# Query weights of the expert heads loaded ahead, and gathers that take row places in the order in which they come free

## The chip, the cores and the metric

The kernel runs on one core of a Trainium2 chip. Its engines run programs of their own and meet at semaphores: TensorE (PE, matrix products), VectorE (DVE), ScalarE (ACT), GpSimd (POOL) and SyncE (SP), which here only issues DMAs. The DMA engines (16 for the core) move data between the chip's memory (HBM) and on-chip memory. The metric is the device time of one execution in microseconds (us); lower is better.

## The reference, cut to what matters

Two transformer blocks run over 256 tokens of width 1024 in float32. The change touches only the end of the second block, a feed-forward layer that picks single experts (PEER): eight heads, each of which chooses 16 of 16384 experts for every token.

```python
P_HEADS, N_KEYS, P_KEY_DIM, P_TOPK, P_CHUNK = 8, 128, 256, 16, 128

def peer_ffn(x, w_q, sub_keys, expert_u, expert_v):
    q = _rms((xt @ w_q).reshape(T, P_HEADS, P_KEY_DIM))
    s1 = einsum('thd,hnd->thn', q[..., :half], sub_keys[:, 0])
    s2 = einsum('thd,hnd->thn', q[..., half:], sub_keys[:, 1])
    v1, i1 = top_k(s1, P_TOPK)
    v2, i2 = top_k(s2, P_TOPK)
    cand = (v1[..., :, None] + v2[..., None, :]).reshape(T, P_HEADS, P_TOPK * P_TOPK)
    vals, ci = top_k(cand, P_TOPK)
    e = take(i1, ci // P_TOPK) * N_KEYS + take(i2, ci % P_TOPK)
    g = softmax(vals)
    a = einsum('cd,ckd->ck', xc, expert_u[ec])
    w = g * gelu(a)
    return einsum('ck,ckd->cd', w, expert_v[ec])
```

`h + peer_ffn(rmsnorm(h))` is the output.

## The kernel before, in words

The blocks ahead of the expert layer stay as they are. In the expert layer the work is cut into 16 **units**: unit u belongs to head u // 2 and to tile t = u % 2 of 128 tokens. A unit has 16 **rows**: row k is one gather, an indirect DMA that POOL issues and that brings, for each of 128 tokens, the 8 KB of its k-th expert (the vectors u and v side by side, `peer_uv`): 1 MB. A row goes through the engines so: VectorE takes the dot product of its u part with the tokens (`dot`, L2880); after four rows ScalarE makes the gelu (`gelu_of`, L1695) and VectorE the weights (`weights_of`, L2890); ScalarE scales an identity matrix by each weight (`diagonals`, L1683); PE multiplies it with the v part and adds it up in PSUM (`add_experts`, L949), and signals `v_used`.

A row lies in one of 16 **places** of 2048 floats per partition (`slots`): 0 and 13 to 15 in arena_u, 1 in uv_proj, 2 and 3 in uv_mk, 4 to 7 in ring, 8, 11 and 12 in arena_v, 9 and 10 in uv_gain. Before, row k of every unit lies in place k, so the gather of row k waits for row k of the unit before. Places 4 to 7 hold the output projection's weights until PE signals `w_out_used` (twice, one count for two places), place 12 the sub-keys until they are turned, place 8 the first head's query weights.

The choice of experts for unit u + 1 is made on VectorE between the dot products of unit u (`first_eights` to `name_experts`), and `experts_ready` lets POOL issue its gathers. For a head's first tile it needs the scores of the next head: PE computes the queries of that head for both tiles from its **query weights** (1 MB, `peer_wq`), ScalarE copies and squares them, PE makes sums of squares and key scores (`key_scores`, L934, L939, after row 5 of an even unit), VectorE signals `ms_ready`, and POOL makes the scale (`power`, L1905) after its gather of row 9 of the odd unit.

Query weights: the first head's go to place 8; those of heads 1 to 3 (`early_wq`) to places 13 to 15, loaded before the layer begins, and PE computes the queries of all three (`early_queries`, L919) before its first row, which frees these places for rows 13 to 15 of unit 0. Heads 4 to 7 share one region of arena_v that is no place (`late_wq`): SP loads the next after PE has used the last (`late_wq_used`, L490), and PE computes their queries in units 6, 8, 10 and 12 (`key_queries`). PE and ScalarE write out the first six units and run units 6 to 13 as a loop; VectorE and POOL write out two and run 2 to 13 as a loop; the last two are written out.

Order is set by each engine's program alone: POOL issues gathers in order of rows, and whatever a gather waits for holds up all that stands behind it on POOL.

## Time and profile before

| | us |
|---|---|
| median of 3 runs | 1421.2 (1420.14 to 1421.49) |
| the profiled execution | 1421.38 |
| its span, first to last instruction | 1419.6 |
| first gather issued | 759.30 |
| dot product of the last row | 1412.00 |
| PE busy | 1295.4 (91%) |
| VectorE busy | 952.7 (67%) |
| ScalarE busy | 548.9 (39%) |
| POOL busy | 371.1 (26%) |

The profile is of one execution. "x4" after a line counts the instructions that it merges; a bracket at its end says how long the engine stood idle before and what ended that. PE's products in float32 are recorded in two passes, so one row is four records. "From issue to landing" of a DMA is the time until its data has arrived. Line numbers are those of the kernel before.

### The profile page before, as it was taken

What the parts mean: (1) busy time and instruction counts of PE and PEld (TensorE: products, weight loads), DVE (VectorE), ACT (ScalarE), POOL (GpSimd) and SP (SyncE); (2) the same over time, 40 slices, a digit from 0 to 9 for tenths busy, and PEclk for the clock granted to TensorE, in tenths of its full rate; (3) what the DMA queues carried; (4) which work ended last, traced back from release to release, by engine and by line L of the source; (5) the groups of instructions that cost most, each with busy time, mean ns of one, the idle gap of its engine ahead of it and who ended that gap; (6) DMA issues with size and microseconds to landing.
All of it is one profiled execution on the core that took longest, in us unless ns stands there. A gap on an engine that the chain in (4) does not pass through costs nothing.

```text
span 1419.6 us, 18216 instructions
## 1 busy us (share of the span) xinstructions
PE 1295.4 (91%) x5858; PEld 882.7 (62%) x5858; DVE 952.7 (67%) x2302; ACT 548.9 (39%) x1135; POOL 371.1 (26%) x392
## 2 busy tenths in 40 slices
PE   7999999999999999999999988887878879788778
PEld 6998888878978888878776633333433435343333
DVE  4577566675676665685746787777767677777755
ACT  4674444445655444455742322212222222122221
POOL 0104000000000000012804455444444444434440
PEclk9999999999999999999999999899999999999999
DMA  9815665546325565465335999999999999999997
GB/s 358 307 63 160 195 194 177 177 149 240 116 90 178 178 190 194 159 227 175 121 119 223 420 420 421 420 422 422 422 420 421 422 421 421 422 422 421 421 421 306
DMA packets 96962, 406.63 MB, mean 286 GB/s; under 512 B 6891, under 2 KB 43948, under 8 KB 60172
## 3 DMA queue, kind: packets, MB, share of 16 engines
q0 software_dynamic: 39552, 276.60, 47.4%
q1 hardware_dynamic: 57356, 129.34, 26.6%
q8 instruction: 31, 0.51, 0.1%
q14 instruction: 23, 0.19, 0.0%
HBM read 404.84 MB, written 1.07 MB: 286 GB/s over the span
## 4 chain that ended last, share of the span: by engine, by line
PE 54%; DMA 23%; DVE 9%; issue 8%; POOL 4%; ACT 2%; DVEq 0%; SPq 0%; POOLq 0%; ACTq 0%
DMA uv_proj<-in_peer_uv,prob 17%; PE ps_up L835 8%; PE ps L775 6%; PE ps L949 6%; PE ps L776 6%; PE ps L777 6%; PE ps_up L837 4%; DMA arena_u<-in_peer_uv,prob 3%; PE ps_up L775 3%; PE ps_up L777 3%; PE ps_up L776 3%; PE ps L1019 2%; DMA ring<-in_peer_uv,prob 2%; PE ps_up L919 1%; POOL small L1905 1%
## 5 line engine op out<-in xcount | busy, mean ns | idle before, releaser
L2177 DVE TENSOR_TENSOR w_low<-ring,w_high 128x1024 fp32r<-128x1024 f32 x140 | 165.3, 1221 | 47.2 <-ACT w_high L1367 39.9
L835 PE MATMUL ps_up<-hT_both,w_high 128*128 128x512 f32 x512 | 182.2, 399 | 0.9 <-DVE hT_both L2170 0.9
L949 PE MATMUL ps<-arena_u,sco 128*128 128x512 f32 x256 | 131.9, 663 | 39.5 <-ACT sco L1683 39.5
L1367 ACT ACTIVATE w_high<-ring 128x1024 fp32r<-128x1024 f32 x140 | 140.3, 1052 | 69.9 <-PE ps L777 69.9
L949 PE MATMUL ps<-arena_v,sco 128*128 128x512 f32 x192 | 101.0, 654 | 48.0 <-ACT sco L1683 48.0
L1683 ACT ACTIVATE sco<-const,prob 128x128 f32<-128x128 f32 x256 | 85.2, 392 | 153.1 <-DVE prob L2890 129.3
L837 PE MATMUL ps_up<-hT_both,w_low 128*128 128x256 f32 x512 | 143.8, 281 | 0.0
L1695 ACT ACTIVATE prob<-prob 128x4 f32<-128x4 f32 (+2 forms) x67 | 13.8, 206 | 319.5 <-DVE prob L2880 319.5
L1911 POOL TENSOR_SCALAR small<-small 128x1 f32<-128x1 f32 x8 | 4.2, 525 | 485.6 <-ACT arena_v L1399 485.4
L949 PE MATMUL ps<-ring,sco 128*128 128x512 f32 x256 | 117.9, 610 | 9.8 <-ACT sco L1683 9.8
L2880 DVE CUSTOM_DVE_ANT_0 arena_u<-arena_u,nat 128x1024 f32<-128x1024 f32 x64 | 78.0, 1225 | 67.6 <-DMA arena_u<-in_peer_uv,prob 67.6
L949 PEld LDWEIGHTS ps<-arena_u,sco 128*128 128x128 f32 x256 | 52.7, 210 | 109.8 <-issue 60.5
L2086 POOL DMA_INDIRECT arena_u<-in_peer_uv,prob x64 | 73.6, 1150 | 169.5 <-PE ps L949 119.7
L835 PEld LDWEIGHTS ps_up<-hT_both,w_high 128*128 128x128 f32 x512 | 96.2, 188 | 24.9 <-DVE hT_both L2170 1.3
L949 PEld LDWEIGHTS ps<-arena_v,sco 128*128 128x128 f32 x192 | 36.7, 202 | 105.2 <-ACT sco L1683 69.4
L837 PEld LDWEIGHTS ps_up<-hT_both,w_low 128*128 128x128 f32 x512 | 96.6, 189 | 1.2
L775 PE MATMUL ps<-w_high,act_high 128*128 128x512 f32 x240 | 94.5, 394 | 0.0
L776 PE MATMUL ps<-w_low,act_high 128*128 128x512 f32 x240 | 94.1, 392 | 0.0
L949 PEld LDWEIGHTS ps<-ring,sco 128*128 128x128 f32 x256 | 48.6, 195 | 73.0 <-issue 54.2
L777 PE MATMUL ps<-w_high,act_low 128*128 128x512 f32 x240 | 93.7, 390 | 0.0
L2880 DVE CUSTOM_DVE_ANT_0 arena_v<-arena_v,nat 128x1024 f32<-128x1024 f32 x48 | 58.6, 1224 | 43.0 <-DMA arena_v<-in_peer_uv,prob 43.0
L2880 DVE CUSTOM_DVE_ANT_0 ring<-ring,nat 128x1024 f32<-128x1024 f32 x64 | 78.4, 1225 | 9.2 <-DMA ring<-in_peer_uv,prob 4.7
(520 smaller groups left out, 2834.5 us busy)
## 6 DMA issues: line engine op xcount, KB each, us to landing
ring<-in_w_up SPq DMA_DIRECT2D x32, 1024.0 KB, 5.5
ring<-in_w_down SPq DMA_DIRECT2D x32, 1024.0 KB, 4.8
qkring<-in_qk_a SPq DMA_DIRECT2D x8, 1024.0 KB, 8.5
qkring<-in_qk_b SPq DMA_DIRECT2D x8, 1024.0 KB, 5.2
ring<-in_w_in SPq DMA_DIRECT2D x8, 860.0 KB, 5.8
...
```

What stands on the lines that cost most here:

```text
L775: pe.matmul(dst, a[0], b[0], start=start, stop=False, skip_group_check=True)
L776: pe.matmul(dst, a[0], b[1], start=False, stop=False, skip_group_check=True)
L777: return pe.matmul(dst, a[1], b[0], start=False, stop=stop, skip_group_check=True)
L835: pe.matmul(ps_up[:, 2 * b + fb, :].rearrange("p (a s) -> p a s", a=2), high, hT_both[:, :, c, :], start=(c == 0), stop=False, skip_group_ ...
L837: last = pe.matmul(ps_up[:, 2 * b + fb, S:2 * S], low, hT_high[:, c, :], start=False, stop=(c == NB - 1), skip_group_check=True)
L949: last = pe.matmul(ps[2 * t + n][:, :], diag[:, k % N_DIAG, :], slots[k][:, D + n * HALF:D + (n + 1) * HALF], start=(first and k == 0), st ...
L1019: last = pe.matmul(ps[k][:, :], hT[:, c, t * P:(t + 1) * P], ring[:, w_out_slots[c // 2], at:at + HALF], start=(c == 0), stop=(c == NB - 1 ...
L1367: sc.activation(w_split[pair][0][:, part], ring[:, slot, part], ACT.Copy)\
L1683: sc.activation(diag[:, k % N_DIAG, :], ident, ACT.Copy, scale=weight[:, 16 * t + k:16 * t + k + 1])\
L2086: po.indirect_dma_start(slots[k], None, T["peer_uv"], bass.IndirectOffsetOnAxis(ap=expert[:, 16 * t + k:16 * t + k + 1], axis=0))\
L2177: ve.tensor_tensor(w_split[pair][1][:, part], ring[:, slot, part], w_split[pair][0][:, part].bitcast(F32), ALU.subtract)\
L2880: ve.tensor_tensor_reduce(row, row, nat[:, t, :], 1.0, 0.0, ALU.mult, ALU.add, dots[:, k:k + 1])\
```

## The change

The weights of heads 4 to 7 are no longer loaded one after the other into one region. Head 4's go to `late_wq`, those of 5, 6 and 7 to places 0, 1 and 2, and all are issued right after those of heads 1 to 3; the last two wait until attention has weighed its values. The gathers start with ten places (`FIRST_PLACES`) and take the others, and used ones, in the order in which they come free (`row_places`, worked out when the program is built): heads 1 and 2 have their queries computed ahead of the first row, heads 3 to 7 in units 1 to 5. Since places no longer repeat with the unit, eight units are written out on VectorE and POOL (then a loop of units 8 to 13), and all sixteen on PE and ScalarE. Copies of the queries of heads 1 to 4 are kept in four places of their own, then reused in turn.

```diff
+FIRST_PLACES = (3, 4, 5, 6, 7, 12, 11, 8, 9, 10)
+QUERY_PLACES = {1: 13, 2: 14, 3: 15, 5: 0, 6: 1, 7: 2}
+QUERY_UNITS = {1: 3, 2: 4, 3: 5, 4: 6, 5: 7}
+N_AHEAD = 2
+N_KEPT = 4
+N_VARIED = 8
+
+def row_places():
+    freed = [("query", j, QUERY_PLACES[j]) for j in range(1, N_AHEAD + 1)]
+    taken = [("start", n, place) for n, place in enumerate(FIRST_PLACES)]
+    for u in range(N_UNITS):
+        for k in range(TOPK):
+            while len(taken) <= u * TOPK + k:
+                taken.append(freed[len(taken) - len(FIRST_PLACES)])
+            freed.append(("row", u * TOPK + k, taken[u * TOPK + k][2]))
+            if k == 1 and QUERY_UNITS.get(u) in QUERY_PLACES:
+                freed.append(("query", QUERY_UNITS[u], QUERY_PLACES[QUERY_UNITS[u]]))
+    return taken
...
-            sp.wait_ge(sem("wq_landed"), count.take("wq_landed", 16 * N_EARLY))
-            for j in range(N_EARLY + 1, P_HEADS):
-                if j > N_EARLY + 1:
-                    sp.wait_ge(sem("late_wq_used"), count.take("late_wq_used"))
-                sp.dma_start(late_wq, T["peer_wq"][j]).then_inc(sem("wq_landed"), 16)
+            sp.dma_start(wq_of[4], T["peer_wq"][4]).then_inc(sem("wq_landed"), 16)
+            sp.dma_start(wq_of[5], T["peer_wq"][5]).then_inc(sem("wq_landed"), 16)
+            count.skip("weighed", 16)
+            sp.wait_ge(sem("weighed"), count.take("weighed", 8))
+            sp.dma_start(wq_of[6], T["peer_wq"][6]).then_inc(sem("wq_landed"), 16)
+            sp.wait_ge(sem("weighed"), count.take("weighed", 2))
+            sp.dma_start(wq_of[7], T["peer_wq"][7]).then_inc(sem("wq_landed"), 16)
...
+            def unit(u):
+                j = QUERY_UNITS.get(u)
+                if j:
+                    queries(j, (0,), wait=j in (4, 6))
+                add_experts(u, range(2))
+                if j:
+                    queries(j, (1,), wait=j in (4, 6))
+                add_experts(u, range(2, 6))
+                if u % NT == 0 and u < N_UNITS - NT:
+                    pe.wait_ge(sem("key_scores_taken"), count.take("key_scores_taken"))
+                    key_scores(u // NT + 1)
+                add_experts(u, range(6, TOPK))
...
-                pe.wait_ge(sem("wq_landed"), count.take("wq_landed", 16 * N_EARLY))
-                for n in range(N_EARLY):
-                    early_queries(n)
...
+                pe.wait_ge(sem("wq_landed"), count.take("wq_landed", 16 * (N_EARLY + 4)))
+                for j in range(1, N_AHEAD + 1):
+                    queries(j, wait=(j > 1))
+                for u in range(N_UNITS):
+                    unit(u)
...
+                if u in QUERY_UNITS:
+                    keep_queries(QUERY_UNITS[u])
                 gelu_of(4, 8)
                 diagonals(t, range(4, 6))
-                if queries:
-                    take_queries()
...
+            def place_free(u, k):
+                what, j, _ = places[u * TOPK + k]
+                if what == "row":
+                    po.wait_ge(sem("v_used"), count.take("v_used"))
+                else:
+                    po.wait_ge(sem("peer_q_done"), count.take("peer_q_done", 4 if j == 5 else 2))
+                alone()
```

POOL issues all gathers. This is its order from the first gather on, before: four gathers into places 0 to 3, of which only the first waits, and four into the ring's.

```order
L2086 DMA arena_u<-in_peer_uv,prob 128x2048 [waits experts_ready]
L2086 DMA uv_proj<-in_peer_uv,prob 128x2048
L2086 DMA uv_mk<-in_peer_uv,prob 128x2048 x2
L2086 DMA ring<-in_peer_uv,prob 128x2048 [waits w_out_used]
L2086 DMA ring<-in_peer_uv,prob 128x2048
L1905 TENSOR_TENSOR small<-small 128x1 [waits ms_ready]
L2086 DMA ring<-in_peer_uv,prob 128x2048 [waits w_out_used]
L2086 DMA ring<-in_peer_uv,prob 128x2048
```

After, to the seventh gather:

```order
L2085 DMA uv_mk<-in_peer_uv,prob 128x2048 [waits experts_ready]
L2085 DMA ring<-in_peer_uv,prob 128x2048 [waits w_out_used]
L2085 DMA ring<-in_peer_uv,prob 128x2048
L2085 DMA ring<-in_peer_uv,prob 128x2048 [waits w_out_used]
L1903 TENSOR_TENSOR small<-small 128x1 [waits ms_ready]
L2085 DMA ring<-in_peer_uv,prob 128x2048
L2067 TENSOR_SCALAR small<-small 128x1 [waits squares_summed]
L2069 TENSOR_SCALAR small<-small 128x1
L1903 TENSOR_TENSOR small<-small 128x1 [waits mean_ready]
L2085 DMA arena_v<-in_peer_uv,prob 128x2048 [waits keys_turned]
L2085 DMA arena_v<-in_peer_uv,prob 128x2048
```

What moved: one gather instead of four goes ahead of w_out_used, and the sixth and seventh follow the turned keys instead of standing behind the first head's queries.

Further on in POOL's first unit, before, from the first head's weights (arena_v) to the first gather of unit 1:

```order
L2086 DMA arena_v<-in_peer_uv,prob 128x2048 [waits experts_ready,peer_q_done]
L1905 TENSOR_TENSOR small<-small 128x1 [waits ms_ready]
L2086 DMA uv_gain<-in_peer_uv,prob 128x2048 [waits keysT_ready,rows_scaled]
L2086 DMA uv_gain<-in_peer_uv,prob 128x2048
L2086 DMA arena_v<-in_peer_uv,prob 128x2048 x2
L2086 DMA arena_u<-in_peer_uv,prob 128x2048 [waits peer_q_done] x3
L2086 DMA arena_u<-in_peer_uv,prob 128x2048 [waits experts_ready,v_used]
```

After, from the same gather on:

```order
L2085 DMA arena_v<-in_peer_uv,prob 128x2048 [waits peer_q_done]
L1903 TENSOR_TENSOR small<-small 128x1 [waits ms_ready,experts_ready]
L2085 DMA uv_gain<-in_peer_uv,prob 128x2048 [waits keysT_ready,rows_scaled]
L2085 DMA uv_gain<-in_peer_uv,prob 128x2048
L2085 DMA arena_u<-in_peer_uv,prob 128x2048 [waits peer_q_done] x2
L2085 DMA uv_mk<-in_peer_uv,prob 128x2048 [waits v_used]
L2085 DMA ring<-in_peer_uv,prob 128x2048 [waits v_used] x3
L2085 DMA ring<-in_peer_uv,prob 128x2048 [waits experts_ready,v_used]
```

What moved: two gathers instead of three wait for queries (peer_q_done), and v_used is waited for from row 12 of unit 0 on instead of from row 0 of unit 1 on.

PE's start of the expert layer, before: queries of three heads (L919, sixteen products each), then the first row (L949), in arena_u.

```order
L919 MATMUL ps_up<-hT,arena_u 128x256 [waits wq_landed,keysT_ready]
L919 MATMUL ps_up<-hT,arena_u 128x256 x15
L919 MATMUL ps_up<-hT,arena_u 128x256 [waits pq_ready]
L919 MATMUL ps_up<-hT,arena_u 128x256 x7
L919 MATMUL ps_up<-hT,arena_u 128x256 [waits pq_ready]
L919 MATMUL ps_up<-hT,arena_u 128x256 x7
L919 MATMUL ps_up<-hT,arena_u 128x256 [waits pq_ready]
L919 MATMUL ps_up<-hT,arena_u 128x256 x7
L919 MATMUL ps_up<-hT,arena_u 128x256 [waits pq_ready]
L919 MATMUL ps_up<-hT,arena_u 128x256 x7
L949 MATMUL ps<-arena_u,sco 128x512 [waits diag_ready]
L949 MATMUL ps<-arena_u,sco 128x512
```

After (queries are L939, rows L965): queries of two heads, then the first row, which lies in uv_mk.

```order
L939 MATMUL ps_up<-hT,arena_u 128x256 [waits wq_landed,keysT_ready]
L939 MATMUL ps_up<-hT,arena_u 128x256 x15
L939 MATMUL ps_up<-hT,arena_u 128x256 [waits pq_ready]
L939 MATMUL ps_up<-hT,arena_u 128x256 x7
L939 MATMUL ps_up<-hT,arena_u 128x256 [waits pq_ready]
L939 MATMUL ps_up<-hT,arena_u 128x256 x7
L965 MATMUL ps<-uv_mk,sco 128x512 [waits diag_ready]
L965 MATMUL ps<-uv_mk,sco 128x512
```

What moved: the sixteen products of head 3 left the front, for unit 1.

SP's end of the program, before:

```order
L480 DMA arena_v<-in_peer_wq 128x2048 [waits hidden_done]
L485 DMA arena_u<-in_peer_wq 128x2048 [waits wq_landed,m_turned_a,c_out]
L485 DMA arena_u<-in_peer_wq 128x2048 x2
L490 DMA arena_v<-in_peer_wq 128x2048 [waits wq_landed]
L490 DMA arena_v<-in_peer_wq 128x2048 [waits late_wq_used] x3
L492 DMA out_y<-h 128x1024 [waits y_ready]
```

After:

```order
L508 DMA arena_v<-in_peer_wq 128x2048 [waits hidden_done]
L513 DMA arena_u<-in_peer_wq 128x2048 [waits wq_landed,m_turned_a,c_out]
L513 DMA arena_u<-in_peer_wq 128x2048 x2
L514 DMA arena_v<-in_peer_wq 128x2048
L515 DMA arena_u<-in_peer_wq 128x2048
L518 DMA uv_proj<-in_peer_wq 128x2048 [waits weighed]
L520 DMA uv_mk<-in_peer_wq 128x2048 [waits weighed]
L522 DMA out_y<-h 128x1024 [waits y_ready]
```

What moved: no load of query weights waits for a matmul of the expert layer any more.

## Rows read from the trace of the kernel before

**Rows 1.** Stretches: busy time of each engine, PE's clock, DMA share, GB/s.
```profile
742.00:759.00 17.00, 17.00 (x76) 10.27 (x75) 7.35 (x35) 3.94 (x12) 0.92 (x3) 1.00 0.00 0
...
760.00:780.00 20.00, 18.65 (x104) 14.24 (x103) 13.19 (x50) 6.51 (x18) 13.91 (x17) 1.00 0.95 380
...
900.00:950.00 50.00, 42.28 (x82) 17.45 (x83) 37.52 (x107) 11.39 (x32) 19.52 (x18) 0.87 1.01 421
```

**Rows 2.** Gathers by source line: the first, the twelfth, all of 860 to 1380.
```profile
L2086 POOL DMA_INDIRECT arena_u<-in_peer_uv,prob x1: 1119/1119/1119, 759.3 to 759.3; - x1
DMA to landing us min/median/max: 6.1/6.1/6.1
...
L2086 POOL DMA_INDIRECT arena_v<-in_peer_uv,prob x1: 1907/1907/1907, 779.4 to 779.4; - x1
DMA to landing us min/median/max: 14.5/14.5/14.5
...
DMA to landing us min/median/max: 18.1/25.1/28.6
```

**Rows 3.** VectorE in time: scores scaled for unit 2's choice, and last dot.
```profile
817.99 0.87 DVE L2731 TENSOR_SCALAR sco<-ps_up,small 128x256 f32<-128x256 f32 x2 [1.61 <-POOL small L1905]
...
1412.00 1.22 DVE L2880 CUSTOM_DVE_ANT_0 arena_u<-arena_u,nat 128x1024 f32<-128x1024 f32 x1 [0.76 <-DMA arena_u<-in_peer_uv,prob]
```

**Rows 4.** SP in time: start, us from first start to last end, what, count.
```profile
722.01 1.28 SPq L485 DMA_DIRECT2D arena_u<-in_peer_wq  x3
731.80 463.32 SPq L490 DMA_DIRECT2D arena_v<-in_peer_wq  x4
...
1030.54 0.33 SPq L490 DMA_DIRECT2D arena_v<-in_peer_wq  x1
...
1112.65 0.33 SPq L490 DMA_DIRECT2D arena_v<-in_peer_wq  x1
```

**Rows 5.** VectorE in time around the load of 1030.5 us: dot products of rows.
```profile
1034.23 1.23 DVE L2880 CUSTOM_DVE_ANT_0 arena_v<-arena_v,nat 128x1024 f32<-128x1024 f32 x1 [1.26 <-DMA arena_v<-in_peer_uv,prob]
...
1039.21 1.23 DVE L2880 CUSTOM_DVE_ANT_0 arena_v<-arena_v,nat 128x1024 f32<-128x1024 f32 x1 [3.75 <-DMA arena_v<-in_peer_uv,prob]
```

**Rows 6.** DMA queues, from the page: packets, MB, share of 16 engines.
```profile
q8 instruction: 31, 0.51, 0.1%
```

**Rows 7.** PE in time: start, us, engine, line, operation, tiles, count.
```profile
762.28 3.68 PE L1019 MATMUL ps<-ring,hT 128*128 128x512 f32 x8
...
774.71 20.89 PE L919 MATMUL ps_up<-hT,arena_u 128*128 128x256 f32 x96
795.43 1.88 PE L949 MATMUL ps<-arena_u,sco 128*128 128x512 f32 x4
797.15 1.88 PE L949 MATMUL ps<-uv_proj,sco 128*128 128x512 f32 x4
...
828.01 3.55 PE L949 MATMUL ps<-arena_u,sco 128*128 128x512 f32 x4 [3.17 <-ACT sco L1683]
831.40 1.88 PE L949 MATMUL ps<-uv_proj,sco 128*128 128x512 f32 x4
```

**Rows 8.** POOL in time: start of expert phase and unit 1, with what ended waits.
```profile
764.60 0.94 POOL L2086 DMA_INDIRECT ring<-in_peer_uv,prob  x1 [0.30 <-issue]
...
770.90 0.57 POOL L1905 TENSOR_TENSOR small<-small 128x1 f32<-128x1 f32 x1
...
776.25 1.60 POOL L2086 DMA_INDIRECT uv_gain<-in_peer_uv,prob  x1 [0.18 <-issue]
...
789.50 0.95 POOL L2086 DMA_INDIRECT arena_u<-in_peer_uv,prob  x1 [5.25 <-PE ps_up L919]
...
798.12 1.50 POOL L2086 DMA_INDIRECT arena_u<-in_peer_uv,prob  x1 [0.77 <-PE ps L949]
...
817.23 0.73 POOL L1905 TENSOR_TENSOR small<-small 128x2 f32<-128x2 f32 x1
```

**Rows 9.** ScalarE in time: the first four scaled identities.
```profile
786.14 1.28 ACT L1683 ACTIVATE sco<-const,prob 128x128 f32<-128x128 f32 x4 [2.42 <-DVE prob L2890]
```

209 lines of the change are left out of this document (89 added, 120 removed).

## Prediction

> **What bounds the kernel now.** I read the table of stretches first. Between the loads of query weights and the first gather the DMA engines are idle (742 to 759 us: 0 GB/s); from 760 us they are full, and they stay full at 421 GB/s (share 1.01): 900 to 950 us is shown, and each stretch from 840 to 1380 us reads within 2 GB/s of it. PE, the busiest engine, has holes and loses clock in them (0.87) [rows 1]. So the last 660 us are a pipe: 256 gathers of 1 MB and whatever else is put into it. One gather costs 2.49 us: 1.049 MB at 421 GB/s. The first was issued at 759.3 us and landed 6.1 us later, at 765.4 [rows 2]; the last was landed when its dot product began, 1412.0 us [rows 3]. Between these lie 255 steps of 2.487 us (634.2 us) and 12.4 us more.
>
> Then SP's own queue: seven query weights (1 MB each) follow the first head's. Three go at 722.0 us, one at 731.8, and three inside the full stretch, at 1030.5, 1112.7 and 1194.8 us (731.80 + 463.32 less its own 0.33) [rows 4]. What one costs there is seen on VectorE: its dot products wait for rows and start 2.49 us apart, but 1034.23 and 1039.21 are 4.98 us apart, one step more [rows 5]. That is 3 x 2.49 = **7.5 us** of the 12.4. The store of half the output near 1398 us (0.5 MB) takes 1.2; 3.7 us are left. Of these I know only that they come in small steps; code loading (31 packets of 16 KB on one queue over the whole run) shares the engines [rows 6].
>
> Why the pipe never runs dry: a row's place is taken from its issue until PE has added it. From 860 us on a gather waits 18.1 to 28.6 us from issue to landing, against 6.1 us with nothing ahead [rows 2]: at least 12 us of rows, about five, are queued ahead of it. Sixteen places are more than the steady pipe needs. The start is thinner. PE runs three heads' queries (20.9 us from 774.71) before the first row is added at 795.43 [rows 7], so the first place comes free only at 797.3, and the next gather takes it at 798.12 [rows 8].
>
> **The change part by part.** The sum is made against the profiled execution: span 1419.6 us, time 1421.4, so 1.8 lie around the span; the median of the runs is 1421.2.
>
> *Three loads leave the full stretch:* -7.5 us. All seven loads are now issued one after the other from 722.0 us: five in a row (12.5 us, to about 735), the sixth and seventh after attention's last weighings, near 734 us (5 us and a latency more, to about 742). The first gather is not issued before 759.3 us: 17 us of idle DMA cover them, and PE's wait for all seven stands at 774.71 us. If that cover were gone, each would push the first gathers by 2.49 us and the gain would be nil.
>
> *Fewer places at the start.* Ten, then one for each of two queries (12), a thirteenth in unit 1, the next in units 3, 4 and 5; 16 from there. A unit is 16 rows (gathers) for one tile of 128 tokens; gathers are numbered from 0 through the units. I go through the places that can be late, with the rule the rows give: a gather lands at the later of its slot in the pipe and its issue + 6.1 us.
> - Gather 1 needs what gather 4 waited for, which went at 764.60 without waiting for PE ("issue") [rows 8]. The second count of w_out_used comes when PE has done its eight records from 762.28, at 766.0 [rows 7]; gather 3 then lands by 772.3, slot 772.9. Gather 5 stands behind the second tile's scale (made by 770.90 + 0.57 [rows 8]) and is the closest: 771.8 + 6.1 = 777.9 for a slot of 778.9, counting the 1.1 us that the landings now slip between the first and the twelfth. Gathers 8 and 9 stand behind rows_scaled and keysT_ready, which let a gather go at 776.25 [rows 8]: by 778.5, for slots of 786.4 and 788.9. Nothing is lost, by a microsecond.
> - Gather 10 takes the place of head 1's weights, used at 781.7 us: no delay. Gather 11 takes head 2's. Four halves of 3.48 us end at 788.6, and POOL issued the gather behind that event at 789.50 [rows 8]. 789.5 + 6.1 = 795.6; its slot, where the twelfth lands now, is 779.4 + 14.5 = 793.9 [rows 2]. **Late by 1.7 us.**
> - Gather 12 needs row 0 added. Without head 3's queries in front, PE begins at 788.6 instead of 795.4: the four scaled identities that it needs are made from 786.14 on, in 1.28 us, and wait for PE now [rows 9]. Row 0 is added by 790.5, the gather goes 0.8 us later [rows 8] and lands at 797.4 for a slot of 798.1. Rows follow every 1.72 us [rows 7] against 2.49 a slot, so the queue grows again.
> - Unit 1 is the second thin place. VectorE begins the choice of unit 2's experts when POOL has made the scale of the scores (817.23 [rows 8]; VectorE at 817.99 [rows 3]), and behind that choice the weights of row 16 come late: PE adds it from 828.01 to 831.56, the first matmuls after a pause being slow [rows 7]. In the changed order POOL's step stands behind gather 25, which takes the place of row 13 instead of row 9. Row 9 is added by 814.4 (795.43, ten rows of 1.72 and 1.8 of scores) and row 13 by 821.3; in the changed order, with PE 6.8 us ahead and one short wait for the weights of row 4, row 13 is added at about 815.5. So row 16 keeps its time, and gather 28, now on its place, goes at 832.4 and lands at 838.5; slot: 765.4 + 28 x 2.487 + 1.1 + 1.7 = 837.8. **0.7 us.** Gather 30 waits for head 3's second half, 3.48 us after row 17 (833.2), so 836.7, issued 837.5, landed 843.6 for 843.5: **0.1 us.**
> - Gathers 31 and 32 take the places of rows 18 and 19, added at 838.4 and 840.1, and land by 845.3 and 847.0 for 846.1 and 848.6; from there the queue grows by 0.77 us a row. From 860 us on three places fewer take at most 3 x 2.49 = 7.5 us off a gather's wait: 18.1 - 7.5 = 10.6, above 6.1 [rows 2]. In unit 3 the same POOL step is behind row 44 instead of row 41, some 8 us later, so VectorE chooses about 2 us later: covered by the 4.5 us between 10.6 and 6.1.
>
> Start in all: +2.5 us. From nearest rows its bounds are 0 (event and issue come 1.7 us sooner) and 7 (both thin places as slow as PE's half-clock rows, below).
>
> *Queries in other units:* a head's queries cost 6.96 us of PE (a third of the 20.89), seven times before as after. Units 1 to 5 hold 16 x 1.72 + 6.96 + 1.75 (scores) = 36.2 us against 39.8 us of gathers: covered. On ScalarE one square of 512 replaces two of 256, nothing.
>
> *Eight units written out:* about 455 more VectorE rows and 220 more PE rows in the order, all to be loaded during the full stretch. By bytes it is under 0.5 us; by the 3.7 us that the present small steps make, up to 2. I take +0.5. Here the Trainium skill ("Runtime: NRT & Kernel Launch", Instruction fetch mechanics) says that crossing into the next block of code is mostly hidden, so that the term would be 0; the rows show packets, not who waits for them.
>
> A second page of the Trainium skill speaks on the size of the first term: "DMA: Bandwidth & Descriptors" (Where 436 GB/s comes from) has the HBM side bind loads to SBUF at about 358 GB/s. The rows show 421, and the measured number decides; by the page a load would be 2.93 us (an estimate) and the three 8.8, so the sum 1.3 us lower.
>
> The end is unchanged: the last row lands, and 7.6 us later the span is over. Sum: -7.5 + 2.5 + 0.5 = **-4.5 us**, 1421.4 - 4.5 = 1416.9 us; counted from the median 1416.7. I take **1416.8 us**.
>
> **The rivals.**
> 1. *The full 7.5.* The waits at the start are absorbed, because POOL's issue follows its event sooner than 0.9 us or a short queue lands faster than 6.1. For: four estimates within 1 us of their slots. Against: [rows 2] has the only landing without a queue. 1413.9 us.
> 2. *Unit 1 starves.* PE stands idle some 6 us before row 16; now it also does a half query between rows 17 and 18, and if it is still at the lower clock (1.2 GHz), 3.48 becomes 6.96 and rows 16, 17 cost 1.7 more each: gathers 28 to 31 come 4 us later. For: row 16 took 3.55 us after a pause of 3.2 [rows 7]. Against: the next row, from 831.40, took 1.88 again [rows 7]. -4.5 + 4 = -0.5, 1420.9 us.
> 3. *Code loading* delays the slowest DMA engine by as much as the steps of now, several times: +3 instead of +0.5. 1419.4 us.
> 4. *Slower than before.* POOL's scale step, behind gather 25, waits for row 13. Should PE not be ahead (the weights of rows 4 to 7 late on ScalarE, which now stands at the queries' copies before the second gelu), row 13 is added at 821.3 as now, the step comes 5 us later, row 16 and gathers 28 on too: +5. Unit 2's rows then land late in a pipe with 13 places, whose loop (row freed, gather, dot, weight) gives back only part: +3 by half of it. -4.5 + 8 = +3.5, 1424.9 us. It decides when row 13 is added later than about 821 us. Against: 6.7 us of queries are gone from the front.
> 5. *It does not do what it says:* the three loads filled holes, so nothing is won. The step of 4.98 us and the share of 1.01 nearly exclude it. -4.5 + 7.5 = +3, 1424.4 us.
>
> **How the numbers follow.** Forecast (-2.9 to -6.3): 0.62. Rival 1: 0.14. Rival 2: 0.10. Rival 3: 0.08. Rivals 4 and 5: 0.06. A measurement of this kernel tells about 0.2% (2.8 us) from no change. Faster by more: forecast, rival 1 and a part of 3: 0.78. Within: rivals 2 and 3: 0.16. Slower: 0.06. The range goes from 1413.4, the full gain, to 1420.4, which leaves out rivals 4, 5 and half of 2.
>
> **What would show it.** In the changed profile: no load of query weights after 745 us, and no dots 4.98 us apart; first gather still near 759.3 and landed near 765.4; PE's first row near 788.6; a gap of about 1.7 us before the twelfth landing and one below 1 us near 838; DMA share 1.0 from 860 us; the last dot near 1407. The forecast is wrong if the share falls below 0.97 in any stretch after 850 us, if PE's first rows are not earlier, or if the spacing of landings grows with the loops written out.

## The result, and the profile after

The changed kernel is slower: a median of 1423.9 us (1422.4 to 1425.4, 13 runs) against 1420.8 (1419.6 to 1421.5, 13 runs), ratio 1.0022 (95% interval 1.0015 to 1.0029), some 3.1 us more. The forecast was 1416.8 us with a range to 1420.4. In the profiled executions the span goes from 1419.6 to 1421.6 us. So some 7 us are to be found. The time of an execution is longer than its span: by 1.8 us in the kernel before and in the same kernel written out (below), by 2.4 us in the changed kernel (medians of their runs). So 0.6 of the 3.1 us lie outside the span. No trace reaches there, and what they are stays open.

The page of the changed kernel: span, then of the 40 slices the GB/s, then the queues of the DMA engines that load code (packets, MB, share).

```profile
span 1421.6 us, 17639 instructions
...
GB/s 354 305 68 158 194 197 177 177 148 239 118 90 178 179 192 190 165 222 180 115 208 222 402 392 422 421 420 421 421 420 422 420 421 421 422 421 420 422 421 260
...
q8 instruction: 35, 0.57, 0.2%
q14 instruction: 30, 0.25, 0.0%
```

Two slices at the start of the expert layer read 402 and 392; those behind them read 420 to 422, but for the last. The stretches of [rows 1], and two between, tell it more closely.

```profile
742.00:759.00 17.00, 17.00 (x76) 10.34 (x75) 8.10 (x39) 3.94 (x12) 1.55 (x4) 1.00 0.00 0
760.00:780.00 20.00, 18.65 (x106) 14.69 (x105) 12.80 (x43) 6.51 (x18) 12.25 (x14) 1.00 0.97 355
780.00:800.00 20.00, 19.02 (x69) 12.00 (x68) 19.20 (x58) 6.05 (x17) 7.83 (x7) 1.00 0.98 386
...
836.00:848.00 12.00, 12.00 (x32) 5.75 (x31) 7.75 (x16) 3.94 (x12) 7.78 (x7) 1.00 0.95 354
848.00:856.00 8.00, 8.00 (x20) 3.60 (x19) 4.86 (x17) 4.41 (x9) 5.99 (x5) 1.00 1.01 405
900.00:950.00 50.00, 46.11 (x130) 24.85 (x129) 42.13 (x137) 11.97 (x32) 25.34 (x21) 0.97 1.01 421
```

The pause of 742 to 759 us is still empty, so the seven loads are covered. From 760 to 780 us 355 GB/s were moved, not 380 [rows 1], and the pipe runs thin three times. Read also the share beside the GB/s: 0.97 with 355. Where few rows are queued, some packets take longer (of the 8 KB packets of 770 to 780 us one in a hundred took over 1.5 us, of those of 900 to 950 us none over 1.0; the usual time is 0.31 us), and all of that time counts in the share. The share hides such a loss; the GB/s show it.

SyncE's queue after: no load of query weights stands behind 725.25 us (that of head 7; the prediction had the last two near 734 us, which costs nothing here).

```profile
721.09 1.28 SPq L513 DMA_DIRECT2D arena_u<-in_peer_wq  x3
722.41 0.69 SPq L514 DMA_DIRECT2D arena_v<-in_peer_wq  x1
723.15 0.45 SPq L515 DMA_DIRECT2D arena_u<-in_peer_wq  x1
723.65 0.47 SPq L518 DMA_DIRECT2D uv_proj<-in_peer_wq  x1
725.25 0.33 SPq L520 DMA_DIRECT2D uv_mk<-in_peer_wq  x1
```

VectorE in time, where a load stood before [rows 5], and its last dot product, which answers to [rows 3].

```profile
1036.33 1.23 DVE L2892 CUSTOM_DVE_ANT_0 uv_gain<-uv_gain,nat 128x1024 f32<-128x1024 f32 x1 [1.12 <-DMA uv_gain<-in_peer_uv,prob]
1038.81 1.23 DVE L2892 CUSTOM_DVE_ANT_0 arena_u<-arena_u,nat 128x1024 f32<-128x1024 f32 x1 [1.25 <-DMA arena_u<-in_peer_uv,prob]
...
1413.99 1.23 DVE L2892 CUSTOM_DVE_ANT_0 uv_proj<-uv_proj,nat 128x1024 f32<-128x1024 f32 x1 [0.75 <-DMA uv_proj<-in_peer_uv,prob]
```

The step of 4.98 us is gone, yet the last dot stands at 1413.99 us, 1.99 later than before; from there to the end of the span it is 7.6 us, as before. So all of the difference of the spans lies in the pipe of gathers. The trace has all 16 landings of each gather (one for each DMA engine), and the last of the 16 is the gather's landing. Three of them cut the pipe:

| landing of gather, us | before | after | difference |
|---|---|---|---|
| 0 | 765.4 | 764.1 | -1.3 |
| 40 | 866.6 | 871.7 | +5.1 |
| 255 | 1412.0 | 1414.0 | +2.0 |

From gather 0 to 40 the changed kernel loses 6.4 us (107.6 against 101.2), where the forecast had 2.5. From 40 to 255 it wins only 3.2 us (542.2 against 545.4), where three loads had to bring 7.5. There seven steps take 3.44 us instead of 2.49 (two before). Each stands beside a packet of 8 KB on the code queue q14:

| q14 packet at, us | 910.7 | 955.8 | 1022.1 | 1074.3 | 1118.2 | 1166.1 | 1385.9 |
|---|---|---|---|---|---|---|---|
| long step ends at, us | 912.5 | 958.2 | 1023.8 | 1077.0 | 1120.2 | 1168.4 | 1388.0 |

VectorE in time at one of them, and the queue q14 in 1164 to 1169 us:

```profile
1165.01 1.23 DVE L2892 CUSTOM_DVE_ANT_0 arena_u<-arena_u,nat 128x1024 f32<-128x1024 f32 x1 [1.26 <-DMA arena_u<-in_peer_uv,prob]
1168.46 1.23 DVE L2892 CUSTOM_DVE_ANT_0 uv_mk<-uv_mk,nat 128x1024 f32<-128x1024 f32 x1 [2.09 <-DMA uv_mk<-in_peer_uv,prob]
1170.95 1.23 DVE L2892 CUSTOM_DVE_ANT_0 ring<-ring,nat 128x1024 f32<-128x1024 f32 x1 [1.25 <-DMA ring<-in_peer_uv,prob]
...
q14 instruction: 1, 0.01, 0.4%
```

Five other packets of q14 after 890 us (894.2, 972.9, 1068.0, 1104.2, 1248.1) and seven of 16 KB on q8 between 949 and 1351 us have no long step beside them.

The last of the 16 landings and the middle one (the ninth in order of time) tell two different stories, and this separates the two losses:

| gathers, by which landing, us | before | after | before, VectorE's code written out |
|---|---|---|---|
| 0 to 40, middle | 99.7 | 106.1 | 99.9 |
| 0 to 40, last | 101.2 | 107.6 | 101.2 |
| 40 to 255, middle | 544.7 | 537.1 | 544.6 |
| 40 to 255, last | 545.4 | 542.2 | 550.0 |

At the start all 16 landings are late together. In the full stretch the middle landing wins 7.6 us, the whole of three loads, and only the last falls back: the fifteenth landing of the 16 still takes 537.6 us after and 543.9 us with VectorE's code written out, against 543.7 before. So one DMA engine of the 16 is behind, and the others are not. The distance between the first and the last of the 16 stays as it is between the long steps and grows by 0.9 to 1.0 us at each of the seven (2.5, 3.4, 4.3, 5.2, 6.2, 7.2, 8.1 and 8.9 us). The last column is a kernel of the experiments below.

The start, on GpSimd: the waits that [rows 8] has of before.

```profile
758.37 1.12 POOL L2085 DMA_INDIRECT uv_mk<-in_peer_uv,prob  x1 [8.16 <-PE ps L1034]
...
761.10 0.94 POOL L2085 DMA_INDIRECT ring<-in_peer_uv,prob  x1 [0.31 <-issue]
765.93 0.94 POOL L2085 DMA_INDIRECT ring<-in_peer_uv,prob  x1 [3.90 <-PEq L1081]
...
781.66 0.95 POOL L2085 DMA_INDIRECT arena_u<-in_peer_uv,prob  x1 [2.76 <-PE ps_up L939]
788.57 0.97 POOL L2085 DMA_INDIRECT arena_u<-in_peer_uv,prob  x1 [5.96 <-PE ps_up L939]
790.28 1.42 POOL L2085 DMA_INDIRECT uv_mk<-in_peer_uv,prob  x1 [0.75 <-PE ps L965]
...
816.85 0.74 POOL L1903 TENSOR_TENSOR small<-small 128x2 f32<-128x2 f32 x1
...
832.25 0.95 POOL L2085 DMA_INDIRECT ring<-in_peer_uv,prob  x1 [11.66 <-PE ps L965]
```

And what became of four of them, by source line in a stretch that holds one gather each (3, 11, 12 and 28), from issue to landing:

```profile
L2085 POOL DMA_INDIRECT ring<-in_peer_uv,prob x1: 936/936/936, 765.9 to 765.9; - x1
DMA to landing us min/median/max: 8.3/8.3/8.3
...
L2085 POOL DMA_INDIRECT arena_u<-in_peer_uv,prob x1: 966/966/966, 788.6 to 788.6; - x1
DMA to landing us min/median/max: 7.0/7.0/7.0
...
L2085 POOL DMA_INDIRECT uv_mk<-in_peer_uv,prob x1: 1422/1422/1422, 790.3 to 790.3; - x1
DMA to landing us min/median/max: 8.3/8.3/8.3
...
L2085 POOL DMA_INDIRECT ring<-in_peer_uv,prob x1: 948/948/948, 832.2 to 832.2; - x1
DMA to landing us min/median/max: 7.1/7.1/7.1
```

Three thin places, then. By the last landing gathers 1 to 5 lose 3.4 us, 11 to 13 lose 2.3 and 30 to 35 lose 2.6; by the middle landing it is 2.2 us at gathers 1 to 5, 1.8 at 11 to 13 and 2.5 at 28 to 33, against 0.2 us from gather 0 to 40 before. With one or two rows ahead these gathers took 7.0 to 8.3 us, not 6.1. Single steps of the last landing scatter from one execution to the next: the step to gather 1 took between 2.48 and 3.76 us in the kernels below, with the same 1.4 us between the two issues. Code packets fall into the start too, before and after (by the last landing 1.7 us are lost there before). One of 16 KB at 772.2 us stands beside the step of 4.15 us to gather 3 (before: at 773.0, beside 3.50 us to gather 4). This step is not the queue's: with gather 3 issued 3.3 us sooner ("One gather more" below) it takes 4.16 us all the same.

### The profile page after: what moved, and what is told of

Read it like the earlier page. It is cut to its first block, busy times and chain, and to the rows that moved or that the text cites. A ratio compares the mean times of both kernels' runs of the same rounds, so it can differ in the third digit from the quotient of the medians.

```text
span 1421.6 us, 17639 instructions
## 1 busy us (share of the span) xinstructions
PE 1292.5 (91%) x5858; PEld 879.8 (62%) x5858; DVE 953.4 (67%) x2302; ACT 548.4 (39%) x1131; POOL 377.2 (27%) x392
## 4 chain that ended last, share of the span: by engine, by line
PE 56%; DMA 20%; DVE 11%; issue 7%; POOL 4%; ACT 2%; DVEq 0%; SPq 0%; POOLq 0%
DMA uv_mk<-in_peer_uv,prob 14%; PE ps L965 9%; PE ps_up L865 8%; PE ps L805 6%; PE ps L806 6%; PE ps L807 6%; PE ps_up L867 4%; DMA ring<-in_peer_uv,prob 3%; PE ps_up L805 3%; PE ps_up L807 3%; PE ps_up L806 3%; PE ps L1034 2%; DMA arena_v<-in_peer_uv,prob 2%; PE ps_up L939 1%; DMA arena_u<-in_peer_uv,prob 1%
## 5 line engine op out<-in xcount | busy, mean ns | idle before, releaser
L965 PE MATMUL ps<-ring,sco 128*128 128x512 f32 x276 | 135.8, 631 | 36.8 <-ACT sco L1686 36.8
L965 PE MATMUL ps<-arena_u,sco 128*128 128x512 f32 x248 | 124.3, 638 | 36.1 <-ACT sco L1686 36.1
L965 PEld LDWEIGHTS ps<-ring,sco 128*128 128x128 f32 x276 | 53.1, 197 | 108.3 <-issue 60.8
L965 PE MATMUL ps<-arena_v,sco 128*128 128x512 f32 x204 | 99.9, 626 | 17.9 <-ACT sco L1686 17.9
L2085 POOL DMA_INDIRECT ring<-in_peer_uv,prob x69 | 82.7, 1198 | 125.5 <-PE ps L965 92.6
L965 PEld LDWEIGHTS ps<-arena_u,sco 128*128 128x128 f32 x248 | 49.0, 202 | 103.9 <-issue 56.5
L2892 DVE CUSTOM_DVE_ANT_0 ring<-ring,nat 128x1024 f32<-128x1024 f32 x69 | 84.4, 1227 | 39.7 <-DMA ring<-in_peer_uv,prob 38.4
L2085 POOL DMA_INDIRECT arena_u<-in_peer_uv,prob x62 | 70.0, 1129 | 94.8 <-PE ps L965 69.2
L965 PEld LDWEIGHTS ps<-arena_v,sco 128*128 128x128 f32 x204 | 39.2, 199 | 70.7 <-issue 42.2
```

The lines of the kernel that those rows point to most:

```text
L965: last = pe.matmul(ps[2 * t + n][:, :], diag[:, k % N_DIAG, :], slots[place_of(u, k)][:, D + n * HALF:D + (n + 1) * HALF], start=(u < NT a ...
L2085: po.indirect_dma_start(slots[n], None, T["peer_uv"], bass.IndirectOffsetOnAxis(ap=expert[:, 16 * t + k:16 * t + k + 1], axis=0))\
L2892: ve.tensor_tensor_reduce(row, row, nat[:, t, :], 1.0, 0.0, ALU.mult, ALU.add, dots[:, k:k + 1])\
```

## The experiments

The theory: the loads give what was forecast, and two things take it back, VectorE's written-out code in the full stretch and the short queue at the start. Every kernel was timed beside the kernel before, which had medians of 1420.9 us each time; the changed kernel's own median is that of the result. A position that stands without a row below is that of a landing or of a packet in the trace.

### What three loads cost

```diff
                 if j > N_EARLY + 1:
                     sp.wait_ge(sem("late_wq_used"), count.take("late_wq_used"))
-                sp.dma_start(late_wq, T["peer_wq"][j]).then_inc(sem("wq_landed"), 16)
+                    sp.sem_inc(sem("wq_landed"), 16)
+                else:
+                    sp.dma_start(late_wq, T["peer_wq"][j]).then_inc(sem("wq_landed"), 16)
```

> The kernel before, with one edit: the loads of the query weights of heads 5, 6 and 7 are left out (SyncE only counts them as landed), so those heads are chosen with head 4's weights; nothing else moves. Theory: a 1 MB load in the full stretch costs one step of the pipe, 2.49 us, so 3 x 2.49 = 7.5 us less than the kernel before, some 1413.4 us, and no dot products 4.98 us apart. Rival (rival 5 of the prediction): the loads fill holes, and the time is within 1 us of the kernel before.

Measured: 1413.4 us (1412.8 to 1414.3), ratio 0.9948 (0.9934 to 0.9961). VectorE where the load of 1030.5 us had been:

```profile
1035.60 1.23 DVE L2882 CUSTOM_DVE_ANT_0 arena_v<-arena_v,nat 128x1024 f32<-128x1024 f32 x1 [1.26 <-DMA arena_v<-in_peer_uv,prob]
1038.09 1.23 DVE L2882 CUSTOM_DVE_ANT_0 arena_u<-arena_u,nat 128x1024 f32<-128x1024 f32 x1 [1.05 <-DMA arena_u<-in_peer_uv,prob]
```

The price of a load in a full pipe is its bytes at the pace of the pipe: 7.5 us for three, as forecast. Rival 5 falls.

### What written-out code costs

```diff
-                with count.loop(P_HEADS - 1 - N_EARLY, diag_ready=32, key_scores_taken=1, pq_ready=4, wq_landed=16) as i:
+                for i in range(P_HEADS - 1 - N_EARLY):
...
-                with count.loop(P_HEADS - 2, gate_w_ready=2, gelu_ready=8, rms_ready=1, key_scores_done=1,
+                for _ in range(3):
+                    unit(0, more=True)
+                    unit(1)
+                with count.loop(P_HEADS - 5, gate_w_ready=2, gelu_ready=8, rms_ready=1, key_scores_done=1,
```

The first pair of lines is TensorE's (ScalarE's is like it), the second VectorE's (GpSimd's is like it).

> The kernel before, with its units written out as in the changed kernel: all sixteen on TensorE and ScalarE, eight on VectorE and GpSimd; same places, same loads, same order. Theory: the changed kernel's landings show seven steps of 3.44 us instead of 2.49 between 910 and 1388 us where the kernel before shows two, each beside an 8 KB code packet; written out alone, the kernel before should show the same, so 5 x 0.95 = 4.7 us more, some 1425.5 us. Rival (the prediction's term): code loading costs 0.5 us, 1421.3 us, and the long steps of the changed kernel have to do with its places.

Measured: 1426.3 us (1425.7 to 1428.4), ratio 1.0040 (1.0026 to 1.0054): **+5.4 us** for code that computes and moves just what the kernel before does. Its long steps end at 905.7, 953.9, 1019.6, 1075.2, 1118.4, 1171.6 and 1393.8 us, each behind a q14 packet, while its first forty landings take 101.1 us, as before. In its trace gathers 40 to 255 take 4.4 us more (549.8 against 545.4); the other 1.0 us is a first gather that lands later (766.5 against 765.4 us). The term was 0.5 in the sum, up to 2 in its bounds.

Whose code is it? The next two kernels split the edit: VectorE alone, and all the others without VectorE.

> The kernel before, with eight units written out on VectorE alone (then its loop); TensorE, ScalarE and GpSimd keep their loops. The long steps (3.43 us) of the written-out kernel come some 50 us apart up to unit 9 and then stop until unit 15, which is how long VectorE's code is written out there; TensorE's and ScalarE's goes on to the end. Theory: all of the 5.4 us that writing out costs (1426.3 against 1420.9) come from VectorE's code, since its 8 KB packets fall on the DMA engine that is last anyway: 1426.3 us, and the 16 landings of a gather end up 9 us apart. Rival: the cost is shared among the engines by the amount of code, and VectorE alone costs 2 us or less: 1423 us.

> The counterpart: the kernel before with all sixteen units written out on TensorE and ScalarE and eight on GpSimd, VectorE's loop kept. It loads more code than VectorE's eight units do (16 KB packets every 70 us to the end). Theory: this code comes through DMA engines that are ahead of the last one and costs nothing, within 0.5 us of 1420.9 us, with two long steps in the full stretch as before. Rival: every packet of code costs its own time wherever it falls, and the cost is 2 to 4 us: 1423 to 1425 us.

Measured: VectorE alone 1425.3 us (1424.7 to 1426.0), ratio 1.0032 (1.0020 to 1.0044); all but VectorE 1421.5 us (1420.4 to 1422.9), ratio 1.0007 (0.9998 to 1.0016). The code queues of the two from 900 to 1400 us, VectorE alone first:

```profile
q8 instruction: 4, 0.07, 0.1%
q14 instruction: 9, 0.07, 0.0%
```

```profile
q8 instruction: 8, 0.13, 0.1%
q14 instruction: 5, 0.04, 0.0%
```

The two kernels load the same number of packets there, and the second one more bytes (0.17 MB against 0.14), but only VectorE's cost time: 4.4 us against 0.6, and the second interval holds no change. The theory of 5.4 us for VectorE alone and the rival of 2 or less both miss the number; the theory is the nearer by far. In the second kernel one packet of 16 KB (1218.4 us) stands beside a step of 3.11 us, so the others' code is cheap, not always free. The landings say why. Of the 16 landings of gather 250, the last came 4.7 us after the first in the kernel before, 4.4 us with the others' code, 9.1 us with VectorE's, 9.2 us in the changed kernel. A gather is landed when the slowest of the 16 DMA engines is done with its part. A code packet, so the long steps say, delays the engine that it goes through by 0.95 us. On an engine that is ahead of the last one this would not be seen; VectorE's packets come again and again through the one that is last. The trace does not name the engine of a packet. That it is always the same one is concluded, not read: the distance from the first to the last landing grows at each long step (from 2.3 to 8.8 us over seven with VectorE's code alone), while the middle landing keeps its pace (544.6 us for gathers 40 to 255, 544.7 before).

### VectorE's loop two units longer

```diff
+N_VARIED_V = 6
...
-                for u in range(N_VARIED):
+                for u in range(N_VARIED_V):
                     unit(u)
...
-                    unit(N_VARIED)
-                    unit(N_VARIED + 1)
+                    unit(N_VARIED_V)
+                    unit(N_VARIED_V + 1)
```

> The changed kernel with VectorE's loop two units longer: six units written out instead of eight (rows of units 6 and 7 have the places of units 8 and 9 already, so the same instructions serve). Theory: VectorE loads two units less of code, two of the seven long steps between 910 and 1388 us go: 2 x 0.95 = 1.9 us less than 1423.9, some 1422.0 us. Rival: the number of long steps is set by other engines' code, and the time stays 1423.9 us.

Measured: 1422.5 us (1419.9 to 1425.1), ratio to before 1.0012 (1.0003 to 1.0021), 1.4 us less than the changed kernel. In the full stretch, gathers 40 to 255 took 539.1 us instead of 542.2; two long steps (1024.1, 1067.4) and 0.4 us of a third (958.5) are left of six before 1200 us, and the landings of gather 250 are 6.4 us apart. So in this execution the edit is worth 3.1 us in the full stretch, not two steps: with the packet of 912.2 us there is no long step either. The start was 0.5 us longer and the first landing 1.3 us later than in the changed kernel's execution, and the runs scatter more than those of the other kernels. The 1.4 us of the medians have an uncertainty of about as much: the intervals of the two ratios (1.0003 to 1.0021 and 1.0015 to 1.0029) overlap. That VectorE's long steps go is shown by the landings; how much time it is worth, between 1.4 and 3, is open.

### What the places cost

The changed kernel with thirteen places at its start; the loads of heads 5 to 7 are left out for it.

```diff
-FIRST_PLACES = (3, 4, 5, 6, 7, 12, 11, 8, 9, 10)
-QUERY_PLACES = {1: 13, 2: 14, 3: 15, 5: 0, 6: 1, 7: 2}
+FIRST_PLACES = (0, 1, 2, 3, 4, 5, 6, 7, 12, 11, 8, 9, 10)
+QUERY_PLACES = {1: 13, 2: 14, 3: 15}
...
-        wq_of = [first_wq] + early_wq + [late_wq, slots[0], slots[1], slots[2]]
+        wq_of = [first_wq] + early_wq + [late_wq] * 4
```

> The changed kernel with heads 5 to 7 chosen by head 4's query weights, so that three loads are left out and places 0, 1 and 2 are free: the gathers start with thirteen places, four of them before any wait, sixteen from unit 1 on; same code written out. Theory: fewer places cost the changed kernel about 6 us between the first landing and 870 us (2.5 were forecast); with thirteen places that goes, and the time is about 5 us below the changed kernel's 1423.9 (the first gather goes no earlier than there): some 1418.5 us. It is then the written-out kernel less three loads, 1425.5 - 7.5 = 1418. Rival: the places cost only the 2.5 us of the forecast, and the time is 1421.4 us.

Measured: 1417.7 us (1417.2 to 1421.5), ratio 0.9981 (0.9972 to 0.9990). That is 6.2 us below the changed kernel, which loads the same code and has no load in the full stretch either: **the price of three places at the start is some 6 us**, not 2.5. With the places come the waits that hang on them: four gathers go ahead of the first wait here, one in the changed kernel. The two are not told apart by this run. And it is 3.2 us below the kernel before: 7.5 for the loads less 4.4 for VectorE's code. Its first forty landings take 102.1 us, 5.5 less than in the changed kernel (by the middle landing 100.5 against 106.1).

### The scale in unit 1 sooner

```diff
-                unit(u, power_at=9 if u % NT else None)
+                unit(u, power_at=(6 if u == 1 else 9) if u % NT else None)
```

> The changed kernel with one step moved: in unit 1 GpSimd makes the scale of the scores behind its gather of row 6 (gather 22) instead of row 9 (gather 25). VectorE stands idle from 813.3 to 817.6 us for this step, and behind it come the choice for unit 2, the weights of row 16 and gather 28. Theory: VectorE's choice begins some 4 us earlier, gathers 28 to 33 go earlier by as much, and the 2 us that the landings lose between gathers 28 and 33 (3.62, 2.62, 2.85 and 2.75 us a step instead of 2.49) are gone: 1421.9 us. Rival: the scale waits for its sum of squares anyway, or the queue at that place is deep enough, and the time stays at 1423.9 us.

Measured: 1421.3 us (1420.4 to 1423.2), ratio to before 1.0002 (0.9993 to 1.0011), 2.6 us less than the changed kernel. VectorE had stood idle for the scale, 4.28 us in the changed kernel. Now it takes it right behind a dot product. VectorE in time, of the changed kernel and then of this one:

```profile
817.63 0.88 DVE L2742 TENSOR_SCALAR sco<-ps_up,small 128x256 f32<-128x256 f32 x2 [4.28 <-POOL small L1903]
```

```profile
814.18 0.87 DVE L2742 TENSOR_SCALAR sco<-ps_up,small 128x256 f32<-128x256 f32 x2
```

GpSimd in time: the scale is made 4.2 us sooner, and gather 28 goes at 827.00 instead of 832.25 us.

```profile
812.65 0.73 POOL L1903 TENSOR_TENSOR small<-small 128x2 f32<-128x2 f32 x1
...
827.00 1.03 POOL L2085 DMA_INDIRECT ring<-in_peer_uv,prob  x1 [5.16 <-PE ps L965]
```

Its steps from gather 28 to 31 are all 2.49 us, and the stretch of 836 to 848 us reads 420 GB/s instead of 354:

```profile
836.00:848.00 12.00, 11.49 (x28) 4.92 (x27) 5.87 (x12) 4.45 (x9) 7.66 (x7) 1.00 1.02 420
```

One small step that stood behind a wait of GpSimd, which needs nothing of that wait, cost 2.6 us. The profiled execution is the slowest of this kernel's eleven: it shows the place (by the middle landing gathers 28 to 33 lose 0.2 us instead of 2.5), not the total.

### One gather more ahead of the first waits

```diff
-QUERY_PLACES = {1: 13, 2: 14, 3: 15, 5: 0, 6: 1, 7: 2}
+QUERY_PLACES = {1: 13, 2: 14, 3: 15, 5: 0, 6: 1, 7: 11}
-FIRST_PLACES = (3, 4, 5, 6, 7, 12, 11, 8, 9, 10)
+FIRST_PLACES = (2, 3, 4, 5, 6, 7, 12, 8, 9, 10)
...
+            sp.wait_ge(sem("squares_summed"), count.take("squares_summed", 14))
             sp.dma_start(wq_of[7], T["peer_wq"][7]).then_inc(sem("wq_landed"), 16)
```

> The changed kernel with head 7's query weights in place 11 instead of place 2 (two scratch outputs of ScalarE that lay there go elsewhere, and SyncE's load waits for the last of the others, some 735 us instead of 734). The number of places stays ten, but place 2 is free at the start: two gathers go before the first wait for w_out_used instead of one, and every gather up to the sixth goes one slot sooner. Theory: of the 3.4 us that the landings lose between gathers 0 and 5 in the changed kernel (steps of 3.55, 4.15 and 3.42 us) about 1.5 are from the short queue and go; the gap at gather 11 (3.20, 2.93 us) stays or grows by part of it: 1422.9 us, between 1422 and 1423.9. Rival: the first landings are bound by the start of the DMA engines alone and not by the waits, and the time stays at 1423.9 us.

Measured: 1422.9 us (1421.1 to 1424.7), ratio to before 1.0016 (1.0007 to 1.0025), 1.0 us less than the changed kernel. That is the number of the forecast, but the two intervals overlap for the most part (1.0007 to 1.0025, 1.0015 to 1.0029), so the medians alone do not show a gain. The landings do. The first forty take 104.7 us instead of 107.6 in this execution, the fastest of the eleven, and by the middle landing (106.1 and 103.6 us) one sees where: gathers 1 to 5 lose 0.3 us instead of 2.2 (the 1.5 of the theory), gathers 11 to 14 lose 2.9 instead of 1.8, and gathers 28 to 33 lose 1.0 instead of 2.5, which nobody forecast. By the last landing the steps to gathers 1 and 3 are as long as in the changed kernel (3.75 and 4.16 us): that part of the start is not the queue's, as the rival has it, though not for all of the loss. The load of head 7 goes at 735.0 us (725.25 in the changed kernel).

### The three together

> The changed kernel with the three edits of the earlier runs together: the scale in unit 1 behind gather 22, VectorE's loop from unit 6 on, head 7's weights in place 11. If the losses are separate places of one pipe they add up: 1423.9 - 2.6 (scale) - 1.4 to 1.9 (two long steps fewer) - 1.0 to 1.5 (start) = 1418.5 us, between 1417.5 and 1419.5, below both kernels. Rival: the scale and the first places cure the same shortage of rows in the queue (a row won at the start is a row in hand at gather 28), and then the sum is 1419.5 to 1420.5 us.

Measured: **1418.95 us** (1418.35 to 1419.39), ratio to before 0.9985 (0.9976 to 0.9994). The three single edits gave 2.6 + 1.4 + 1.0 = 5.0 us, the three together 5.0, and the rival's 1419.5 to 1420.5 us lie above every run. The sum of the medians does not prove that the places are separate, since 1.4 and 1.0 are hardly clear of noise, and the landings say that two of them are not: from gather 0 to 40 the middle landing wins 1.8 us with the scale alone, 2.5 with place 11 alone and 3.0 with both, not 4.3. The longer loop brings 3.2 us behind gather 40 by the last landing (539.0 against 542.2 us). So the rival has the mechanism in part right (a row won at the start is a row in hand at gather 28) and the total wrong. The version beats both kernels: 2.0 us below the one before, by its interval 0.9 to 3.4, so the sign is sure and the size is not. What is still lost at its start is in steps of 3.87, 3.71 and 3.62 us at gathers 11 to 13.

### How far ahead a gather must be issued

Two kernels took the question out of the start and into the steady pipe.

```diff
             first_unit()
-            unit(1, power_at=9)
+            count.skip("v_used", 6)
+            unit(1, power_at=3)
```

The second kernel has 8 for 6.

> The kernel before, with every gather from unit 1 on waiting for a row that is six rows later than the one whose place it takes, as if there were ten places (and the scale of the scores made behind row 3 of the odd unit, so that it is not held up). A row's place is then taken for 10 x 2.49 = 24.9 us, of which some 14 lie between its landing and its product: some 10 us from issue to landing instead of 25. Theory: the pipe keeps its pace as long as a gather is issued 8 us or more before its slot; some 2.49 us a step in the middle of units, and at most 3 us more in all from unit starts: 1421 to 1425 us. Rival: a shallow queue costs pace by itself: over 5 us more.

> The same with eight rows later, as if there were eight places: 19.9 us for a place, less 14 leaves 6 us from issue to landing, which is the 6.1 us that the first gather takes with nothing ahead. By the rule of the prediction (a gather lands at the later of its slot and its issue + 6.1 us) the pace would just hold, 2.49 us a step, 1421 to 1426 us. Theory: it does not, since two gathers that follow each other with a short queue landed 3.4 to 3.8 us apart in the changed kernel though they were issued 1.7 us apart; with a mean of 7.5 to 8 us from issue to landing each step takes 21.5 to 22 / 8 = 2.7 us, 0.2 us more over 240 steps: some 1470 us.

Measured: ten places 1435.1 us (1432.9 to 1437.2), eight places 1573.8 us (1572.4 to 1575.2). The stretch of 900 to 1400 us, and the gathers of 900 to 1380 us by source line, from issue to landing; ten places first, then eight:

```profile
900.00:1400.00 500.00, 414.92 (x1003) 191.20 (x1002) 352.65 (x1013) 113.85 (x310) 224.42 (x203) 0.94 1.01 420
```

```profile
DMA to landing us min/median/max: 6.2/10.1/12.9
```

```profile
900.00:1400.00 500.00, 369.17 (x843) 169.46 (x842) 288.08 (x832) 92.92 (x255) 177.25 (x165) 0.88 0.90 338
```

```profile
DMA to landing us min/median/max: 5.4/8.2/12.1
```

With ten places the steady pipe keeps its 420 GB/s at 10.1 us from issue to landing, as the theory said. Its total missed the forecast all the same (1435 against 1421 to 1425), since the first gather of unit 1 now waits for row 6 and comes 11.6 us after the one ahead of it: the start was left out of that forecast. With eight places both forecasts are wrong, mine by 100 us: the median of 8.2 us hides that places come free in bunches of four rows (one gelu, one weight step for four), so that gathers come two to four at a time (four from 1070.9 to 1076.1 us, two from 1082.0, four from 1088.9) and then the pipe runs dry. That this is the whole cause is not shown: TensorE's granted clock also reads 0.88 in this stretch, against 0.94 with ten places.

The 2295 gathers after the first in nine of the executions (the two kernels, and all the others in which places, order or loop differ from them) give the rule. A gather's landing is here the middle one of its 16 (the ninth), which code packets hardly touch. Take the time from a gather's issue to the landing of the one before it, and by how much its own landing comes later than 2.487 us after that one:

| issue to the landing before, us | gathers | extra step, mean us | share with over 0.25 us |
|---|---|---|---|
| 0 to 2 | 30 | 1.97 | all |
| 2 to 3 | 40 | 0.44 | 72% |
| 3 to 4 | 86 | 0.44 | 58% |
| 4 to 5 | 93 | 0.26 | 30% |
| 5 to 6 | 119 | 0.01 | 1% |
| 6 to 8 | 218 | 0.00 | 0% |
| 8 and more | 1694 | 0.02 | 2% |

(Fifteen more were issued only after that landing; the 2% of the last line are loads and code. Of the 249 gathers below 5 us 199 are of the two shallow kernels.) From 5 us on nothing is lost, which is 7.5 us before the gather's own slot. The prediction asked for 6.1 us before the slot, that is 3.6 in this table, where more than half of the gathers lose something.

## Why the prediction was wrong, point by point

- **Three loads, -7.5: right.** 1420.9 to 1413.4 us with nothing else changed, and no step of 4.98 us left. That they are covered when issued ahead is right too: 0 GB/s from 742 to 759 us. The Trainium skill's figure ("DMA: Bandwidth & Descriptors", Where 436 GB/s comes from: some 358 GB/s) would have made them 8.8 us, an estimate; the measurement says 7.5, at the pace of 421 GB/s.
- **Eight units written out, +0.5: mis-sized, and the largest error.** It is +4.4 us (VectorE alone) to +5.4 (all engines) by the medians, and 4.6 and 4.4 us in the gathers 40 to 255 of their traces. I weighed bytes, and took the 3.7 us of small steps of the kernel before as an upper guide for all code. What counts is not how much is loaded but which DMA engine it goes through, and whether that is the one that ends last. Rival 3 named the mechanism (the slowest DMA engine delayed several times) but gave it +3 and a chance of 0.08. The prediction named one code queue, q8, and left out the second, which the page of before has too (`q14 instruction: 23, 0.19, 0.0%`) and whose packets stand beside the long steps. The trace of before had what was needed: the 3.45 us step that ends at 897.4 us beside the code packet of 895.0, and one more (1343.7 beside 1341.9) where VectorE's loop ends. The first comes while VectorE runs its loop's code for the first time (unit 3), the second where it leaves the loop (unit 14), and none between: that gives a price for each new stretch of its code.
- **The Trainium skill's rule on that term** ("Runtime: NRT & Kernel Launch", Instruction fetch mechanics: crossing into the next block of code is mostly hidden) agrees with the kernel that has all but VectorE's code written out (0.6 us, and no change within its interval). It fails for VectorE's (4.4 us), whose packets delay the data of all.
- **Fewer places, +2.5: the events right, the rule wrong.** Gather 11 was forecast to land at 795.6 us and did; gather 28 was forecast to go at 832.4 and went at 832.25. But the loss from gather 0 to 40 is 6.4 us, by the last landing as by the middle one. The step that failed is the rule "the later of its slot and its issue + 6.1 us". It was taken from the one gather that had nothing ahead of it and nothing behind. At the thin places a gather behind one or two rows took 7 to 8.3 us, so some count as late that I had passed as in time. By the middle landing these are gathers 4 and 5 (1.1 and 0.9 us; "nothing is lost, by a microsecond"), 12 (1.0), 28 and 29 (0.3 each) and 32 (0.8), beside 11 (0.8) and 30 (1.1). The long steps to gathers 1 and 3 by the last landing are not of this kind, as said above. The bounds of 0 to 7 did hold the value; I took one near the lower end, for no better reason than that the single estimates were small.
- **Rival 2** (unit 1 starves, TensorE at its lower clock) came half true: row 16 took 3.78 us and gathers 30 to 33 lost 2 us, but head 3's half took 3.62 us, so it was not at half its pace; the queue was short before that. **Rival 4** did not happen: the scale was made at 816.85 us, not five later. **Rival 1**, the full gain, would need both errors to be zero.
- **The first gather** went 0.9 us sooner and landed 1.3 us sooner than before. That was not forecast. Since the same gather goes between 758.3 and 760.9 us in the eleven other kernels, whatever they change, I count it as scatter.
- **The steady pipe: right.** From 860 us on the shortest time from issue to landing was forecast at 10.6 us with three places fewer, and is 10.5. The changed kernel's gathers of 860 to 1380 us, by source line:

```profile
DMA to landing us min/median/max: 10.5/23.7/29.6
```

- **The sign I looked for at the end was blind, another was not.** "DMA share 1.0 from 860 us" holds in every stretch, and the last dot is still 7 us later than forecast. A share of 1.01 and 421 GB/s are means over 16 engines; 15 of them run ahead while the last falls behind, 0.95 us at a time. The sign that shows it is the distance between the first and the last landing of one gather, or the step between dot products: 3.44 instead of 2.49 us, seven times in 215. The last sign of the prediction's list, that the spacing of landings grows with the loops written out, is the one that came true.

The sum, redone with what was measured: -1.3 (first landing) + 6.4 (start) - 7.5 (loads) + 4.7 (five long steps more, of 0.95) = +2.3 us, against +2.0 for the spans of the profiled executions. The 0.6 us outside the span come on top, and no term of the prediction stood for them.
